# Expert gates scattered into a DRAM table, and the expert layer in two passes (up-products, then down-products)

## What is computed

```
q   = (h @ wq) split into 8 heads x 2 halves of 64
s   = q against 128 subkeys per half              # 2 x 8 x 128 scores a token
sv, si = top-16 of each half
cand = sums of all 16 x 16 pairs; top-16 again   -> 16 experts a head, 128 a token
gates = softmax over the 16 of a head
y[t] = sum_k gates[t,k] * gelu(h[t] . u[expert k]) * v[expert k]
```

## Time and profile before

| | us |
|---|---|
| times of the runs | 3946.01, 3949.14, 3950.29 |
| span of the profiled execution | 3944.0 |
| PE busy | 3668.8 (93%) |
| DVE busy | 2582.7 (65%) |
| POOL busy | 1645.1 (42%) |
| ACT busy | 732.8 (19%) |
| moved by DMA | 1026.96 MB, mean 260 GB/s |

### The profile page before, as it was taken

The page is one execution under the profiler, slowest core; times in us unless marked ns, Lnnn a source line. Parts: engine busy times, 40 slices in busy tenths (PEclk is TensorE's granted clock), DMA queues, the critical chain, the costliest instruction groups (busy, mean ns, idle before and its releaser), DMA issues. The chain is left out here.

```text
span 3944.0 us, 39966 instructions
## 1 busy us (share of the span) xinstructions
PE 3668.8 (93%) x13726; PEld 2099.9 (53%) x13726; DVE 2582.7 (65%) x5929; ACT 732.8 (19%) x1622; POOL 1645.1 (42%) x1498
## 2 busy tenths in 40 slices
PE   2988888999999999999989887889999999999997
PEld 1545676655555555555445566765555555555543
DVE  5685688777666666677724738878677646556344
ACT  1143355400000000000012535552000000000000
POOL 0030155446556644444502003544777655445340
PEclk7998999999999999999999998999999999999999
DMA  6321234579999999999930131447999999989774
GB/s 218 126 101 46 90 86 145 185 289 405 379 379 369 378 373 378 379 372 353 393 138 2 47 121 54 126 136 256 359 410 410 387 354 354 366 337 359 304 290 160
DMA packets 365386, 1026.96 MB, mean 260 GB/s; under 512 B 30849, under 2 KB 132481, under 8 KB 364417
## 3 DMA queue, kind: packets, MB, share of 16 engines
q0 software_dynamic: 147456, 536.94, 35.5%
q1 hardware_dynamic: 118000, 433.99, 28.9%
q10 hardware_dynamic: 99728, 53.48, 4.8%
HBM read 965.07 MB, written 59.22 MB: 260 GB/s over the span
## 5 line engine op out<-in xcount | busy, mean ns | idle before, releaser
L1859 PE MATMUL ps<-colsT,arena 128*128 128x384 f32 x4096 | 1359.0, 486 | 5.6 <-DMA arena<-in_peer_ut 5.6
L1859 PEld LDWEIGHTS ps<-colsT,arena 128*128 128x128 f32 x4096 | 775.8, 190 | 584.4 <-issue 94.7
L1894 PE MATMUL ps<-arena 128*128 128x512 f32 x1536 | 676.5, 592 | 0.0
L1366 POOL DMA_INDIRECT proj<-in_peer_u,eidx x336 | 478.9, 1425 | 240.9 <-DVE modbc L1560 110.5
L1366 POOL DMA_INDIRECT proj<-in_peer_v,eidx x335 | 361.1, 1078 | 312.7 <-DVE colsT L1571 214.5
L1894 PEld LDWEIGHTS ps<-arena 128*128 128x128 f32 x1536 | 291.8, 190 | 345.2 <-issue 317.6
L1352 POOL TENSOR_SCALAR x<-iota,modbc 128x128 f32<-128x128 f32 x192 | 145.2, 771 | 719.3 <-ACT modbc L1692 551.5
L1560 DVE CUSTOM_DVE_ANT_0 proj<-proj,rows 128x1024 f32<-128x1024 f32 x336 | 399.4, 1222 | 59.0 <-DMA proj<-in_peer_u,eidx 57.2
L1571 DVE SCALAR_TENSOR_TENSOR colsT<-proj,modbc,colsT 128x1024 f32<-128x1024 f32 x330 | 410.1, 1286 | 14.4 <-DMA proj<-in_peer_v,eidx 13.1
L1894 PE MATMUL ps<-arena,rows 128*128 128x512 f32 x768 | 337.8, 592 | 0.0
L1894 PE MATMUL ps<-arena,x 128*128 128x512 f32 x768 | 337.7, 592 | 0.0
(11 more groups left out here) (298 smaller groups left out, 3716.3 us busy)
## 6 DMA issues: line engine op xcount, KB each, us to landing
arena<-in_peer_ut SPq DMA_DIRECT2D x256, 512.0 KB
arena<-in_peer_v SPq DMA_DIRECT2D x256, 512.0 KB
gmat_d<-arena ACTq DMA_DIRECT2D x24, 2048.0 KB, 9.3
arena<-gmat_d SPq DMA_DIRECT2D x64, 768.0 KB
proj<-in_w_adaT SPq DMA_DIRECT2D x48, 512.0 KB
modbc<-in_w_adaT SPq DMA_DIRECT2D x30, 512.0 KB, 3.7
rows<-in_w_adaT SPq DMA_DIRECT2D x18, 512.0 KB, 3.5
arena<-in_w_in SPq DMA_DIRECT2D x2, 4224.0 KB, 16.6
```

What stands on the lines that cost most here:

```text
L1366: pool.indirect_dma_start(ring[slots[at]], None, tab, bass.IndirectOffsetOnAxis(ap=eidx[:, b * SLOTS + q:b * SLOTS + q + 1], axis=0)).then ...
L1859: mm = pe.matmul(ps[:, 2 + j % 2, 0:ND], utab[:, j % UR, k], hT[:, k, NG:T], start=(k == 0), stop=(k == KT - 1))
L1894: mm = pe.matmul(ps[:, Y_BANKS[2 * d + c2], :], wT[j % CR][:, d * P:(d + 1) * P], vtab[:, j % VR, c2 * 512:(c2 + 1) * 512], start=(j == 0) ...
```

## The change

The gate table is no longer multiplied out. A table `gate_d[l]` (128 groups x 128 experts x 384 tokens) is filled with zeros by six DMAs on ACT's queue during the mixer, and POOL then adds the gates into it with 128 indirect DMAs a dense block, each of 128 single words with `compute_op=ADD`. The PEER block has two passes: all 128 up-stages, with the GELU results sent to DRAM (`act_d`), then all 128 down-stages, which load them back. The u and v tables of the gathered blocks lie side by side in DRAM (`peer_uv`), and one gather brings an 8 KB row of both: 256 gathers a layer, in a ring of 9 slots (5 from pair 76 on), two rows in arrears for the sum (`LAG`). The first 84 of the 256 pairs (`N_U`) are worked off in the up-pass from stage 42 on (`PAIR_J`), the rest in the down-pass. The 48 modulation tiles of layer 1 all move into the up-pass of layer 0. `place`, `turn`, `scatter_rows`, `spread`, `mark_rows`, `x_d` and `gmat_d` are gone.

Constants and the two tables in DRAM:

```
+UR, AR, VR, WR, GR = 4, 5, 4, 10, 5
+ZERO_JS = 64
+ZERO_DMAS = JBLK // ZERO_JS * 3
...
+    gate_d = [nc.dram_tensor(f"gate_d{q}", (JBLK, P, ND), F32, kind="Internal").ap() for q in range(depth)]
+    act_d = nc.dram_tensor("act_d", (JBLK, P, ND), F32, kind="Internal").ap()
...
+        PAIR_J, N_U, N_WIDE = 42, 84, 76
...
+        EXP_AT = {11: 1, 19: 2, 29: 3, 40: 4}
+        HEADS_FIRST, PAIRS_HEAD = 9, 5
+        ADA_PAIR = [12 + 3 * n // 2 for n in range(NMOD)]
+        ADA_J = [max(PAIR_J + ADA_PAIR[n - 2] + 4, 50) if n >= 2 else 46 for n in range(NMOD)]
...
+        def pairs_upto(j):
+            return min(NPAIRS, N_U + ((NPAIRS - N_U) * (j + 1) + 119) // 120)
```

ACT in the mixer, whose last instruction then is a wait for `g_zeroed`:

```
+                    if ZERO_STEP <= s < ZERO_STEP + ZERO_DMAS:
...
+                        act.dma_start(gate_d[l][j0:j0 + ZERO_JS][:, :, d0:d0 + P].rearrange("j i t -> i j t"),
+                                      zeros[:, :].unsqueeze(1).to_broadcast([P, ZERO_JS, P])).then_inc(g_zeroed, 16)
```

SP in PEER. `keep_hidden(j)` waits for GELU j and sends the hidden tile to `act_d`; `load_g(0)` waits until all scatters of the layer have landed:

```
+                for j in range(JBLK):
+                    keep_hidden(j)
+                    load_u(UR + j)
+                    if l + 1 < depth:
...
+                        for n in range(NMOD):
+                            if ADA_J[n] == j:
+                                load_ada(n)
+                    if j == JBLK - 4:
+                        sp.wait_ge(row_used, N_WIDE)
+                        sp.wait_ge(q_mm, NQ)
+                        for q in range(VR):
+                            load_v(q)
+                        for q in range(WR):
+                            load_hidden(q)
+                for j in range(GR):
+                    load_g(j)
+                for j in range(JBLK):
+                    load_g(GR + j)
                     load_v(VR + j)
...
+                    load_hidden(WR + j)
```

POOL. `scatter(d, h)` waits for the block's routing (h = 0) or for the landing of the head before; `fetch(0)` waits for the routing of block 0 and for the last scores and queries, and every fetch for its slot:

```
+                def scatter(d, h):
...
+                    for q in range(TOPK):
+                        s = b * SLOTS + h * TOPK + q
+                        pool.indirect_dma_start(gate_flat, bass.IndirectOffsetOnAxis(ap=eidx[:, s:s + 1], axis=0),
+                                                gates[:, s:s + 1], None, compute_op=ALU.add).then_inc(g_sent, 16)
...
+                for i in range(len(DB) * PH):
+                    scatter(i // PH, i % PH)
+                    if i >= HEADS_FIRST:
+                        for _ in range(PAIRS_HEAD):
+                            fetch(n)
+                            n += 1
+                while n < NPAIRS:
+                    fetch(n)
+                    n += 1
```

DVE, after the routing of all five blocks. `pair(n)` is `dot(n)` and `add_row(n - 2)`, and the latter waits for `weigh(n - 2)`; `late_dots(m)` waits for modulation tile m:

```
+                for n in range(N_U):
+                    pair(n)
+                    if n == 3:
+                        gated(NB - 1)
+                    if l + 1 < depth:
+                        for m in range(NMOD):
+                            if ADA_PAIR[m] == n:
+                                late_dots(m)
...
+                for j in range(JBLK):
+                    dve.wait_ge(gm_landed[j % GR], 16 * (j // GR + 1))
+                    dve.wait_ge(act_back[j % WR], 16 * (j // WR + 1))
+                    dve.tensor_tensor(wT[:, j % WR], wT[:, j % WR], gring[:, j % GR], ALU.mult).then_inc(ut_gated, 1)
+                    upto = pairs_upto(j)
...
+                    for n in range(done, upto):
+                        pair(n)
```

ACT in PEER. `weigh(n)` waits for `dot(n)` and makes that pair's coefficient in two operations:

```
+                for j in range(JBLK):
                     gelu(j)
...
+                    if j in EXP_AT:
+                        exps(EXP_AT[j])
+                    if PAIR_J <= j < PAIR_J + N_U:
+                        if j == PAIR_J:
+                            act.wait_ge(routed, 1)
+                        weigh(j - PAIR_J)
+                for n in range(N_U, NPAIRS):
...
+                    weigh(n)
```

PE. The turns, queries and scores of the last blocks stand behind up-stages 0 to 13; `v_stage(0)` waits for all 128 GELUs:

```
+                for j in range(JBLK):
+                    u_stage(j)
...
                 for j in range(JBLK):
-                    u_stage(U_AHEAD + j)
                     v_stage(j)
```

More of the change, by code:

```diff
@@ new lines, in build @@
+        pairs_ring += [region(arena, 8192 + q * 2 * D, 2 * D) for q in range(4)]
+        RING = len(pairs_ring)
+        dots = region(rows, 4 * D, len(GB), SLOTS)
+        coef = region(rows, 4 * D + NG, len(GB), SLOTS)
+        ysum = [hT[:, :, q * P:(q + 1) * P] for q in range(2)]
+        late_junk = region(proj, 6 * D, D)
+        late_ada = [region(proj, q * D, D) for q in (7, 8)]
+        late_silu = [modbc[:, q:q + D] for q in (3 * D, 7 * D)]
+        NPAIRS = len(GB) * SLOTS
+        LAG = 2
@@ L1523, in _, with pair @@
+                def pair(n):
+                    if n < NPAIRS:
+                        dot(n)
+                    if n >= LAG:
+                        add_row(n - LAG)
+                        if (n - LAG) % SLOTS == SLOTS - 1:
+                            close_block((n - LAG) // SLOTS)
                 residual(0)
@@ new lines, in _, with late_dots @@
+                route(1, 1)
+                mean(4)
+                route(1, 2)
+                normed(4)
+                route(1, 3)
+                gated(0)
+                for k in range(1, NB):
+                    for step in range(4 if k == 1 else 0, STEPS - 1):
+                        if k > 1 and step == 4:
+                            gated(k - 1)
+                        route(k, step)
+                dve.wait_ge(g2_landed, 16)
+                def late_dots(n):
+                    if n == 0:
+                        dve.wait_ge(silu_landed, 32)
+                    dve.wait_ge(w_landed[n % 2], 16 * (n // 2 + 1))
+                    ada_dots(dve, c, l + 1, n, late_ada[n % 2], late_silu, late_junk)
@@ new lines, in gelu, with weigh @@
+                    act.activation(hidden[:, j % AR], ps[:, u_bank(j), 0:ND], ACT.Gelu).then_inc(ut_gelu, 1)
+                def weigh(n):
+                    i, q = n // SLOTS, n % SLOTS
+                    b = GB[i]
+                    one = dots[:, i, q:q + 1]
+                    act.wait_ge(dot_made, n + 1)
+                    c.link(act.activation(one, one, ACT.Gelu))
+                    act.activation(coef[:, i, q:q + 1], one, ACT.Copy,
+                                   scale=gates[:, b * SLOTS + q:b * SLOTS + q + 1]).then_inc(coef_made, 1)
```

588 lines of the change are left out of this document (198 added, 390 removed).

## The result

The change makes the kernel slower: median 4649.49 us of four runs (4637.94 to 4655.89) against 3949.72 for the kernel before, ratio 1.1768 (95% interval 1.175 to 1.1786). The forecast was 4117 us with a range of 3860 to 4430; the sign was right, the time is 532 us off and outside the range. What happened is the mechanism of rival B: scatters cost far more than gathers.

A forecast was written before the change was run, and what follows sets the result against it. PE was taken to bound the kernel, with DMA as second resource. The terms sum as 3944 - 300 + 209 + 200 + 46 + 10 + 3 = 4112 us on the profiled span, 4117 as median; range 3860 to 4430.

The forecast's parts named there:

- rival B: POOL's scatters dearer than gathers, 2.0 to 2.5 us each; 4420 to 4760 us, middle 4590; chance 0.13.
- Term 4: POOL's issues: scatters at 1.3 us each with the gap delay the up-passes, +46 us in all.
- Term 2: Layer 0's up-pass: modulation tiles load late, landing time L = 6 us, +209 us.
- the ring: Layer 0's up-pass: a modulation tile's load waits for GELU, weigh and the dot behind the tile's own dots; +209 us.
- Term 5: Waits at each change of pass, +10 us in all; zeroing DMAs hidden under the mixer's end but for +3.
- Term 1: PE's work in two passes: 1472 us a layer against 1622, -300 us, if nothing else sets the pace.
- Term 3: Down-pass transfers: 2.42 MB a stage at 410 GB/s, 5.90 us against 5.16; +100 us a layer, +200.
- Rival C: A lower DMA ceiling for mixed rows, 354 GB/s, a down-pass of 836 us; 4269 us in all; chance 0.07.
- Rival A: Transfers land cheaply: L = 3.5 us and +25 us a layer in the down-pass; 3852 us, faster; chance 0.18.
- The signs named in the forecast: Among them: DVE waits for layer 0's modulation tiles some 46 times, 4 to 6 us; POOL's scatters take 1.0 to 1.3 us.
- the last of the three conditions for being wrong: On POOL: the forecast called itself wrong if scatters take 2 us.

The follow-up runs named there:

- plain scatters: Changed kernel with the same 768 scatters writing instead of adding, so one gate is kept where two heads name the same expert; 4257 us.
- half_and_early: Changed kernel with gates 9 to 16 of each head left out in the dense blocks and modulation tiles loaded two stages earlier; 3998 us.
- tiles_early: Changed kernel with the modulation tiles of layer 0's up-pass loaded two stages earlier; 4511 us.
- half_early_zeros: Changed kernel with half of the dense blocks' gates left out, modulation tiles two stages earlier, zeros issued by SP at PEER's begin; 3916.1 us, ratio 0.9916 to the kernel before.
- three_mended: Changed kernel with zeros at PEER's begin, modulation tiles two stages earlier, first head of each dense block written plainly; 4397.04 us, ratio 1.1134 to the kernel before.

## Why the prediction was wrong

**Term 4 failed, in size: "No row shows a scatter; the nearest is the gather, as both write 128 descriptors. I take 1.3 us each with the gap".** It costs 1.86 with the gap while nothing runs beside it, as POOL's timeline shows (one scatter at 870.91, the next at 872.76), and 1.98 on average:

```profile
870.91 1.55 POOL L1365 DMA_INDIRECT gate_d<-gates,eidx  x1 [0.30 <-issue]
872.76 1.55 POOL L1365 DMA_INDIRECT gate_d<-gates,eidx  x1 [0.30 <-issue]
```

The average is higher because an issue is longer while DVE works. Of the 768 scatters, the 413 with no DVE instruction beside them took 1.54 to 1.61 us; the 137 beside a `scalar_tensor_tensor`, mostly `add_row`'s, took 2.02 on average:

```profile
1128.32 1.99 POOL L1365 DMA_INDIRECT gate_d<-gates,eidx  x1 [0.30 <-issue]
```
```profile
1128.82 1.28 DVE L1551 SCALAR_TENSOR_TENSOR colsT<-arena,rows,colsT 128x1024 f32<-128x1024 f32 x1
```

The term's own structure with that price gives most of the result. In layer 1 the first scatter starts at 2917.2 and the first gather at 3252.75, after ten heads:

```profile
3252.75 1.00 POOL L1378 DMA_INDIRECT rows<-in_peer_uv,eidx  x1 [0.30 <-issue]
3254.06 0.95 POOL L1378 DMA_INDIRECT proj<-in_peer_uv,eidx  x1 [0.30 <-issue]
```

That is 335.5 us, 33.6 a head, where the term had 228 (22.8 a head): 108 later. 15 of these were slack before stage 42, and 8 stood in the forecast: 85 more. Then 14 rounds to the last scatter at 3790.0 are 537 us, 38.4 a round against 29.0: 131 more. Together 216 of the 236 that layer 1's up-pass is over its forecast. The 20 left are near the 15 that the term took off for stages that PE is ahead, but no run tests this. Rival B had 340 for the ten heads and 39 a round at 2.0 us a scatter. Its evidence, "For it: nothing in the trace does this", was used as a reason for 0.13, where it should have been one for a wide range: an operation with no row and a different semantics (read, add, write) is not near a gather because it has as many descriptors. That it decides from 1.4 us fits the plain scatters (1.38 us, and a pass of 727); the price itself was wrong.

**Term 2 was right in mechanism and 58 us too small** (267 for 209), by L = 7.2 in place of 6. In half_and_early, with the tiles early, 48 us over PE's work remain; whether they too are waits for tiles is open. In the kernel after, part of it hides: in layer 0 scatters and ring together give 423 over PE's work. Term 4 had the scatters' rounds of layer 0 hide behind the ring wholly; at the measured price they cost 252 alone beside the ring's 219, and only 96 of that overlap.

**Term 5 failed for the zeros**: +77 in place of +3. The cover that it named, the low DMA share of the mixer's end, was there; what was overlooked is that the issue itself can hold ACT. Of the changes of pass (10 forecast), 36 came, 13 of which went with the tiles' ring (tiles_early). The first up-stage came 8 us later than worked out, in both layers; for that there is no experiment.

**Term 1 held**: 694.7 and 694.8 us for an up-pass with no other limit, and 662 to 665 for a down-pass, with 694 and 660 worked out. **Term 3 held**: 753 for 760, at 409 GB/s as in the earlier trace rows. **Rival C** fell with it: rows of 1.5, 4 and 8 KB mixed moved 409 GB/s in the down-pass. **Rival A** fell: L was longer, not shorter, and the down-pass at the middle value. The signs named in the forecast answered: layer 0's DVE waited for tiles 46 times, though 8.4 us each and not 4 to 6, and scatters took 2 us, the last of the three conditions for being wrong.

The Trainium skill, "DMA: Bandwidth & Descriptors", "Rules for kernel authors", states that an accumulating DMA reads its destination first and writes it later, with nothing that holds the bytes in between. No run here shows this. By that rule heads may not overlap here, since two heads of a token may name the same expert, and the kernel waits for the landing after each head.

## What to carry to other kernels

Price an indirect DMA that adds by itself, from a run if no row of it exists: here its issue took 1.55 us of GpSimd where a gather or a plain scatter took 0.95, and the half of the 384 such issues a layer that half_early_zeros leaves out is most of what lies between 0.8% faster (half_early_zeros) and 11% slower (three_mended). Count all issues of an engine against the pass that they must fit into, and ask which engine would be idle while they go out. Give large DMAs of small rows to an engine that has nothing else to do, and follow each load that is issued "just in time" round its ring: in an in-order program it may wait for its own consumer.

## What was not expected of the hardware

- The issue time of an indirect DMA depends on what it does with each word: 1.55 us for 128 additions, 0.96 for 128 writes, 0.94 for 128 v rows of 4 KB, 0.94 to 1.00 for 128 rows of 8 KB (medians). It is longer while DVE works: 2.02 on average for an addition beside `scalar_tensor_tensor`.
- Additions are dear for the DMA engines too. From 850 to 895 us of the kernel after, nothing but 23 scatters is begun, and the share of the DMA engines is 0.22 at 0 GB/s: 0.22 x 45 us x 16 / 2944 words is an estimated 54 ns of one DMA engine a word. A scatter makes 144 packets with the addition and 32 without.
- Zero DMAs of 4 MB held ACT for up to 18.9 us in the issuing instruction, at a DMA share of up to 1.05 and 291 GB/s.
